# A hybrid decoder step: the sample group moved in front of the prompt, its FFN multiplied beside the prompt's last FFN

## What is computed

```python
xn = rmsnorm(h, g_mix)
z, xbc, dt_raw, q, k, v = split(xn @ w_in)          # 1024 x 2312
y_ssd, new_conv, new_ssm = ssd_branch(...)          # conv, SiLU, state scan, gated norm
y_att = swa(...)                                    # window 128, sink logits, T5 bias
h = h + concat(y_ssd, y_att) @ w_out
h = h + cross_attention(rmsnorm(h, g_cross), mem_k, mem_v, w_cq, w_co)   # 4 heads, 256 tokens
hn = rmsnorm(h, g_ffn)
h = h + (silu(hn @ w_gate) * (hn @ w_up)) @ w_down
y = rmsnorm(h, g_final)
```

## Time and profile before

| | us |
|---|---|
| runs | 3247.93, 3249.22, 3255.84 (median 3249.22) |
| the profiled execution | 3253.04 |
| its span | 3251.2 |
| PE busy | 2993.7 (92%) |
| mean granted clock | 0.929 |
| last matmul of the last prompt FFN (start) | 2783.38 |
| sample's first projection matmul | 2826.21 |
| sample's first FFN matmul | 3120.14 |

### The profile page before, as it was taken

One profiled execution on the slowest core, in us unless ns is written; L12 is line 12 of the kernel. 1 busy time (PEld: TensorE's weight loads), 2 busy tenths in 40 slices (PEclk: granted clock), 3 DMA queues, 4 the chain that ended last, 5 costly groups with the idle time before them and its releaser, 6 DMA issues. The chain is left out here.

```text
span 3251.2 us, 35837 instructions
## 1 busy us (share of the span) xinstructions
PE 2993.7 (92%) x13972; PEld 2402.4 (74%) x13972; DVE 1477.7 (45%) x2234; ACT 1149.2 (35%) x1840; POOL 1030.2 (32%) x507
## 2 busy tenths in 40 slices
PE   7976999999999999999989999999779999667898
PEld 5865788877877878778878787788558888565752
DVE  5545655764245556652465566524352222313111
ACT  4554454354233543442245434422332222111100
POOL 2211433333433333334333333343224444410000
PEclk8988999999999999999999999999889999656679
DMA  5355522222335222223352222233313332571256
GB/s 145 111 126 135 139 78 88 72 71 85 97 107 146 78 88 66 78 85 97 114 146 72 85 72 78 78 97 96 118 39 97 98 97 91 148 213 44 65 182 222
DMA packets 493181, 336.64 MB, mean 104 GB/s; under 512 B 58703, under 2 KB 458195, under 8 KB 492998
## 3 DMA queue, kind: packets, MB, share of 16 engines
q1 hardware_dynamic: 488510, 327.94, 34.7%
q10 hardware_dynamic: 1880, 6.34, 0.5%
q0 software_dynamic: 2624, 0.09, 0.1%
HBM read 311.96 MB, written 23.33 MB: 103 GB/s over the span
## 5 line engine op out<-in xcount | busy, mean ns | idle before, releaser
L786 POOL TENSOR_TENSOR w_lo<-w_raw,w_hi 128x1024 fp32r<-128x1024 f32 x400 | 976.6, 2445 | 1787.1 <-ACT w_hi L800 1787.1
L1593 PE MATMUL L<-xa_h,w_hi 128*128 128x512 f32 x1536 | 615.0, 400 | 3.9 <-DVE xa_l L1420 3.9
L1594 PE MATMUL L<-xa_h,w_lo 128*128 128x512 f32 x1536 | 602.7, 392 | 0.0
L1595 PE MATMUL L<-xa_l,w_hi 128*128 128x512 f32 x1536 | 602.3, 392 | 0.0
L800 ACT ACTIVATE w_hi<-w_raw 128x1024 fp32r<-128x1024 f32 x400 | 421.7, 1055 | 462.0 <-PE L L1595 421.5
L1593 PEld LDWEIGHTS L<-xa_h,w_hi 128*128 128x128 f32 x1536 | 291.1, 190 | 76.1 <-issue 11.4
L1595 PEld LDWEIGHTS L<-xa_l,w_hi 128*128 128x128 f32 x1536 | 290.9, 189 | 62.3
L1594 PEld LDWEIGHTS L<-xa_h,w_lo 128*128 128x128 f32 x1536 | 291.5, 190 | 59.8 <-issue 1.0
L1552 DVE TENSOR_TENSOR sg<-sg,L 128x512 f32<-128x512 f32 x88 | 60.5, 688 | 519.9 <-PE L L1595 519.9
L1593 PE MATMUL L<-hid_h,w_hi 128*128 128x512 f32 x704 | 279.9, 398 | 6.9 <-DVE hT L1560 6.9
L1595 PE MATMUL L<-hid_l,w_hi 128*128 128x512 f32 x704 | 274.8, 390 | 0.0
(11 more groups left out here) (495 smaller groups left out, 4434.2 us busy)
## 6 DMA issues: line engine op xcount, KB each, us to landing
w_raw<-in_w_gate_dram SPq DMA_DIRECT2D x88, 512.0 KB, 3.7
w_raw<-in_w_up_dram SPq DMA_DIRECT2D x88, 512.0 KB, 3.8
w_raw<-in_w_down_dram SPq DMA_DIRECT2D x88, 512.0 KB, 3.4
w_raw<-in_w_in_dram SPq DMA_DIRECT2D x56, 512.0 KB, 3.8
xt<-xT_dram SPq DMA_DIRECT2D x56, 256.0 KB, 3.1
wS<-in_w_down_dram SPq DMA_DIRECT2D x11, 1024.0 KB, 4.9
wS<-in_w_gate_dram SPq DMA_DIRECT2D x10, 1024.0 KB, 5.1
wS<-in_w_up_dram SPq DMA_DIRECT2D x10, 1024.0 KB, 5.1
```

Of the source, the lines that this page charges most:

```text
L786: pool.tensor_tensor(w_lo[:, n % RING, 0:w], w_raw[:, n % RING, 0:w], w_hi[:, n % RING, 0:w].bitcast(F32), ALU.subtract)\
L1593: pe.matmul(acc, wh, rh, start=(k == 0), stop=False)
L1594: pe.matmul(acc, wl, rh, start=False, stop=False)
L1595: last = pe.matmul(acc, wh, rl, start=False, stop=(k == kn - 1))
```

## The change

The numbers of lines in this section's rows are those of the changed kernel, where they are of it.

1. A phase `front` runs first: the sample up to its third norm in one phase instead of three. The projections, `w_out` and `w_co` have the 64 tokens stationary and rows of weights moving, up to 512 columns (w_in in 8 slabs of full rows, 2312 columns). `w_cq` keeps weights stationary. Cross PV has the probabilities stationary (128 x 32) and memory V moving, 512 columns. The state's update and the transposes of memory K are cut into pieces that stand between other stages. The gathers of bias rows by POOL are 16 DMAs in place of 80. At its end it stores h (`hs_dram`) and the normed x (`xs_dram`). Constants, parameters and the bias rows are made here.
2. In the last FFN of the prompt, each tile of a panel gets one more matmul between L1594 and L1595: the raw fp32 slab, stationary, by the sample's 64 tokens (`xsl` for gate and up, `hidS` for down), into PSUM tensor G, banks 0 and 1, 4 and 5. ACT makes `gS` (Silu), DVE `hidS` and sums `yF`. From that FFN on the raw slabs have a ring of 6 and come free when PE is done with them. The old tail's 13 transposes stand behind panels 2 and 6 of this FFN.
3. Behind the last panel, 8 transposes bring `yF` to token rows, and the sample's last norm is put among the prompt's. The tail phase and the three sample phases are gone.
4. `x_before`: in blocks 1 to 3 the x tiles stand one panel later (the first four) and two panels later (the rest).
5. At the start of `main`, SP loads no parameters and doesn't wait for the bias rows.

```diff
+    LAST = pos[("F", NBLK - 1, ffn_steps()[0])]
+    XRAW = 2 * RING
+
+    def raw_place(n):
+
+        return n % RING if n < LAST else RING + (n - LAST) % XRAW if (n - LAST) % XRAW < RING else (n - LAST) % XRAW - RING
...
-            x_before.append(w0 + (4 if b == 0 else 3) if j < XR else min(w0 + use[j - XR][0] + 4, NPAN))
+            x_before.append(w0 + 4 if j < XR else min(w0 + use[j - XR][0] + (4 if b == 0 else 6), NPAN))
...
                 def load_panel(n):
-                    if n >= RING:
+                    if n >= LAST + XRAW:
+                        sp.wait_ge(s["lin_out"], first_out[n - XRAW + 1])
+                    elif n >= LAST + RING:
+                        sp.wait_ge(s["lo_ready"], LAST)
+                    elif RING <= n < LAST:
                         sp.wait_ge(s["lo_ready"], n - RING + 1)
...
-                        sp.wait_ge(s["rsb"], 1)
-                        sp.dma_start(bias_rows.ap(), rrow[:]).then_inc(s["rows_out"], 16)
-                        sp.wait_ge(s["rows_out"], 16)
...
                             act.activation(sg[:, f % 3, :], bank(bank_of[o]), ACT.Silu).then_inc(s["ev_A"], 1)
+                            if not more:
+                                if f >= 2:
+                                    act.wait_ge(s["S_hid"], f - 1)
+                                act.activation(gS[:, f % 2, :], G[:, 0, 0:S], ACT.Silu).then_inc(s["S_g"], 1)
...
-                for c in range(C):
-                    put_y(NBLK - 1, c)
+                put_y(NBLK - 1, 0)
+                put_y(NBLK - 1, 1)
+                act.wait_ge(s["S_h"], 1)
+                act.activation(youtS[:], hrowS[:], ACT.Square, accum_out=nrmF[:, 0:1]).then_inc(s["S_sq"], 1)
+                put_y(NBLK - 1, 2)
+                put_y(NBLK - 1, 3)
...
+                            if not more:
+                                dve.wait_ge(s["S_g"], f + 1)
+                                dve.tensor_tensor(hidS[:, f % HID, :], gS[:, f % 2, :], G[:, 1, 0:S], ALU.mult)\
+                                   .then_inc(s["S_hid"], 1)
...
                             pe.matmul(acc, wh, rh, start=(k == 0), stop=False)
                             pe.matmul(acc, wl, rh, start=False, stop=False)
+                            if side is not None:
+                                to, xs = side(m, k)
+                                pe.matmul(to, raw_of(n)[:, c0:c0 + P], xs, start=(k == 0), stop=(k == kn - 1))
                             last = pe.matmul(acc, wh, rl, start=False, stop=(k == kn - 1))
```

More of the change, by code:

```diff
@@ L140, in panel_dmas @@
     return out
[L143 to L183, removed]
 def rsqrt(dve, v, r, t):
@@ L465, in build @@
+        names = ([f"w_in{r}" for r in range(XRAW)] + [f"xt_in{r}" for r in range(XR)]
+                 + ["hi_ready", "lo_ready", "lin_out", "ev_A", "ev_D", "made", "consts",
+                    "x0_in0", "x0_in1", "x0_in2", "x0_in3", "bias_in", "mem_in", "ssq", "mem_ok",
                     "slab_in0", "slab_in1", "slab_in2", "slab_in3", "piece", "piece_ev", "turned", "bias_ev", "xT0_out", "km_hi", "km_lo",
@@ L626, in build @@
             STEPS = ffn_steps()
+            down_index = {step[1:]: d for d, step in enumerate(step for step in STEPS if step[0] == "down")}
             def unit(b, u):
@@ L1564, in _ @@
                                     final_gain(b, n - 1)
+                            if not more:
+                                d = down_index[f, m]
+                                src = G[:, 4 + d % 2, 0:outs * S].rearrange("p (i t) -> p i t", t=S)
+                                out = yF[:, m * outs:m * outs + outs, :]
+                                if f == 0:
+                                    dve.tensor_copy(out, src).then_inc(s["S_y"], 1)
+                                else:
+                                    dve.wait_ge(s["S_y"], d)
+                                    dve.tensor_tensor(out, out, src, ALU.add).then_inc(s["S_y"], 1)
+                        if not more and p in (4, 8):
+                            last_rows(p == 8)
                         if p >= 1:
@@ L1788, in cross, with last_rows @@
                         yield
+                def last_rows(second):
+                    if not second:
+                        for i in range(4):
+                            last = pe.transpose(G[:, 2, i * P:i * P + P], state[:, i * P:i * P + P], ident[:])
+                        last.then_inc(s["tail"], 1)
+                    else:
+                        pe.wait_ge(s["tail_sb"], 2)
+                    for i in range(4):
+                        j = i + 4 if second else i
+                        last = pe.transpose(G[0:3, 2 if second else 3, i * P:i * P + P], carry[:, j, :], ident[:])
+                    last.then_inc(s["tail"], 1)
+                    if second:
+                        pe.transpose(G[:, 3, 0:P], klast[:], ident[:]).then_inc(s["tail"], 1)
                 def turn_y(b, c):
@@ L1937, in build @@
-        prompt.close()
-        panels = weight_panels(w_in, w_out, w_cq, w_co)
-        NPAN = len(panels)
-        first_out = [sum(p[2] for p in panels[:n]) for n in range(NPAN + 1)]
-        PAN_XBC, PAN_K, PAN_V, PAN_Q, PAN_Z, PAN_OUT = 0, 8, 9, 10, 14, 18
-        PAN_CQ, PAN_CO, PAN_FFN = 26, 30, 34
-        SR = 8
-        sslot = {}
-        on_slot = [0] * SR
-        for n, (parts, _, _) in enumerate(panels):
-            on_slot[n % SR] += sum(KV if part[0] == "kv" else 1 for part in parts)
-            sslot[n] = on_slot[n % SR]
```

1640 lines of the change are left out of this document (792 added, 848 removed).

## The result

| | predicted | measured |
|---|---|---|
| the changed kernel, median | 3088 (3050 to 3135) | 3098.85 us (3098.28 to 3103.45) |
| ratio to the kernel before | 0.950 | 0.9539, 95% interval 0.9527 to 0.9551 |
| profiled execution, its span | 3092, 3090 | 3098.28, 3096.5 |

A forecast was written before the change was run, and what follows sets the result against it. PE was taken to set the end nearly everywhere. Front 203 + 2783.8 - 1.5 (start) + 119 (side matmuls) + 1 (transposes) - 36 (x tiles) + 21 (end) = 3090 us span; median forecast 3088, range 3050 to 3135.

The forecast's parts named there:

- What bounds it: Whole kernel: PE sets the end nearly everywhere, so work added to it in the prompt counts in full.
- Side matmuls: Last FFN of the prompt: 528 side matmuls at 0.225 us each add 119 us, all on the path.
- The front: Sample up to its third norm, now run first: adds 203 us, bounds 190 to 291.
- The two waits for DVE: In the front, up to the end of w_out: waits of some 6 us filled by memory K's transposes, 12 us off.
- x tiles: Stage W, blocks 1 to 3: later x tiles remove PE's stalls for w_lo and xb_l, 36 us saved.
- The start of `main`: Start of the main block: SP freed of bias rows and parameter loads, 1.5 us saved (0 to 6).
- The end: Behind the last matmul: sample phases and tail go, 21 us stay (18 to 27).
- The sample's FFN: Moved from the end into the prompt's last FFN: 131 us become 119, so the move is worth 12 us.
- A: Rival: last FFN of the prompt stays at half clock, 3512 us, slower; chance 0.04.
- B: Rival: side matmuls' weight loads hidden under panel matmuls, 56 us for 119, total 3025; chance 0.06.
- C: Rival: the x-tile stalls stay, total 3124 us; chance 0.13.
- D: Rival: the front stays at half clock, 291 us for 203, total 3176; chance 0.07.

The follow-up runs named there:

- side_k0: Changed kernel with only the first side matmul of each output left, 92 of 528: 0.9246, 2998.2 us.
- x_new: Kernel before with the new places of the x tiles and nothing else: 0.9914, 3218.25 us.
- x_old: Changed kernel with the x tiles of blocks 1 to 3 at their old places: 0.9643, 3128.45 us.
- x_rest4: Changed kernel with only the first four x tiles of a block one panel later, the later ones at their old places: 0.9639, 3130.3 us.
- side_end: Changed kernel with each output's side matmuls in a row ahead of its last panel matmul, not one per tile: 0.9529, 3092.0 us.
- front_stat: Changed kernel with 7 of 8 weight slabs of the front's projections done weights stationary, 64 tokens moving: 0.9636, 3127.85 us.
- side_r1: Changed kernel with 436 of 528 side matmuls as single passes of the rounded type instead of two fp32 passes: 0.9396, 3049.3 us.
- wq_row: Changed kernel with the front's w_cq product done tokens stationary, 512 weight columns moving, plus a copy and 4 transposes: 0.953, 3093.24 us.
- wide: Changed kernel, last FFN 576 columns wide as matmuls of 288, sample's tokens included, no side matmuls; with pool_wait and wq_row: 0.9349, 3034.7 us.
- pool_wait: Changed kernel with POOL's first w_lo waiting until DVE has made the main block's first diagonal: 0.9534, 3094.75 us.

## Why the prediction was right, and where it was off

- **What bounds it: right.** PE has no gap in the last FFN, and side_k0 shows that each side matmul taken out shortens the whole by nearly its own time.
- **Side matmuls: right in kind, 4% too cheap.** 119 us by 0.225 each; 0.236 is what the windows give (7.30 less 5.40 us a panel, over 8), and 0.226 to 0.231 the experiment. The row with 1 moving column gave 0.113 a pass; a pass of 64 columns between long matmuls gives 0.12.
- **The front: 6 us too long, and that near only by luck.** To the end of the projections 48 (measured 49.7), to the end of w_out 109 (114.2), to the end of PV 165 (164.4), to the end of the norm 189 (182.7), 203 at the end (197.0, which is the load at 197.8). Three terms were mis-sized by more than that. The two waits for DVE that memory K's transposes were to fill are still there (6.2 and 4.9 us ahead of L1010 and L1076). The 32 passes of PV took 3.7 us, not 13.8. And w_co was left at its old length, though its form changed as that of w_out did (before, then now):

```profile
3098.40 13.92 PE L1978 MATMUL L<-oS,wS 128*128 128x64 f32 x64 [0.52 <-DVE oS L2615]
```
```profile
167.15 7.05 PE L1158 MATMUL G<-fwc,oS 128*64 128x512 f32 x16 [0.80 <-DVE oS L946]
```
These 7 us are the error of the whole; the others cancel.
- **x tiles: right.** 36 forecast, 35.0 by following the matmuls, 28 to 34 by x_new and x_old. x_old and x_new show that the order is the cause, x_rest4 that it is the place of the tiles behind the first four. The chance of 0.13 for stalls that stay was not needed.
- **The start of `main`: nothing gained.** I took 1.5 us off for SP's earlier freedom; it is 1.8 longer. What sets it is how POOL's first two `w_lo` meet the norm's chain on DVE. Now two operations of 0.17 us each take 2.20 and 2.22. Before, the four `diag` operations of the chain took the blow, 3.01 us where they take 0.87 now:

```profile
14.71 3.01 DVE L1157 TENSOR_SCALAR diag<-ident,rx 128x128 f32<-128x128 f32 x4
```
In x_new, which changes nothing there, the same four took 5.12 us and the first panel started at 25.43 in place of 22.95. So the earlier loads gave nothing, and whether they cost 1.8 us isn't shown.
- **Before stage W of block 1: +1.9**, not shown to be an effect of the change. From the first panel to the first of stage W are 916.8 us here, but 907.6 in side_end and 921.4 in side_k0, which differ from the changed kernel in the last FFN alone.
- **Not foreseen: 3.3 us in the cross attention of block 3** (the table above). 1.6 of it come ahead of the `w_co` panels, where the longest wait, for `vm` from DRAM, is 10.1 us in place of 8.6. 1.7 come in these panels, which start at granted clock 0.50 (2552 to 2556 us; 1.00 before, 2385 to 2388). What made the wait longer wasn't tried.
- **The end: right.** 19.8 us behind the last matmul for 21.
- **The sample's FFN: right that its move saves little.** 131 us at the end against 124 beside the prompt. The spans differ by 154.7 us: 448.0 less at the end (467.8 to 19.8), 35.0 less in stage W, and 197.0 + 1.8 + 1.9 + 3.3 + 124.3 more. The 336 us that the prediction set against the front held some 15 us of the prompt's own end, which still stand in the 19.8. So the gain lies in the front, where 321 us became 197, and in the x tiles; the FFN's move is worth 2 us (131 for 124 and 5 more at the end). Nothing of the prompt runs beside the front, as nothing ran beside the sample before, so its new place by itself isn't a gain: what is left out are waits between phases and passes at half clock. Of the 124 us the runs take apart only the projections (29 us, front_stat); no run has the rewritten front at the sample's old place.
- **Rivals.** A (half clock in the last FFN) didn't occur: the clock was full within 12 us of its first panel. Its evidence, short passes at half clock, was sound in itself, as front_stat shows, but among matmuls of 512 columns it doesn't apply. B fell by side_r1: the loads hide by one, not under matmuls of 64 columns. C fell by the waits. D: the front's projections ran at the full clock. Some 66 us of the front did not: the granted clock is 0.50 to 0.54 from 58 to 68, 85 to 92, 95 to 102, 122 to 143 and 177 to 198 us. The fourth of these stretches holds w_cq, with weights stationary, which wq_row shortened; the others were not tried.

## What to carry to other kernels

Price a small matmul that is slipped between large ones by the load it exposes, not by its columns, and ask first whether its columns can ride with the large one's weights: here 64 columns cost 0.24 us a tile as a matmul of their own and 0.12 as part of the matmuls of 288 (wide). Where a token group is small, keep the tokens stationary and let weights move. And look at what stands ahead of a store in a queue that also waits for readers: one line of a table was worth about 30 us. Last, compare a stage in two traces before a difference of 5 us between medians is put down to an edit: side_end seemed to give 7 us and gave 1.4.

## What wasn't expected of the hardware

- The cross PV of the front, 32 passes with 128 x 32 stationary and 512 columns moving, placed on four different groups of 32 columns of the array:

```profile
160.75 3.68 PE L1145 MATMUL G<-memV,pxT 128*32 128x512 f32 x32 [0.74 <-ACT pxT L740]
```
115 ns a pass, where 512 columns in the full width take 430 and a record here lasts 597: some four ran at a time. That was 10 us less than the front's sum had. The Trainium skill ("TensorE: Matmul & The Clock Gate", "Part 3: Packing small matmuls — row/col tiling") says that tiles of the array at different positions run at the same time; the trace agrees, with these 3.68 us.
- Two small DVE operations on 128 x 4 integers took 2.20 and 2.22 us while POOL subtracted on 128 x 1024, and 0.17 without it. In pool_wait, where they ran apart, the length moved to an operation that now ran beside POOL. The Trainium skill ("SBUF — State Buffer", "SBUF: two separate sides") has VectorE and GpSimd take turns at a pair of ports, each for a whole instruction, where the VectorE instruction uses that pair; 2.2 us, about one `w_lo` (2.44 us), agrees with it.
- An fp32 matmul with 128 stationary columns and 64 moving ran at half clock in a row of its own for 56 us, and at the full clock at half the time per pass in rows of 16 between long matmuls (side_end).
